# First projections of both mixers from rows not yet normalised, tokens' norm factors applied when the result is read out; the first layer's end in another order; one quarter of the output stored alone

## The chip, the core and the metric

The program runs on one core of one Trainium2 chip. Its time is the device time of one execution in microseconds (us). The kernel before takes 794.77 us, the median of three runs (793.01 to 795.64). All weights lie in HBM as fp32 and are read once: 240 MB in all.

## The reference

Two layers work on 272 tokens (16 learned meta tokens in front of 256 tokens of input) of width 1024. Each layer is a mixer and then a mixture of experts, both fed by an RMS norm and both added to the residual `h`:

```python
def rms_norm(x, gain):
    y = xf * lax.rsqrt(jnp.mean(xf * xf, axis=-1, keepdims=True) + NORM_EPS)
    return y * gain

# layer 0
p = rms_norm(h, e_norm) @ e_w_in                      # 1024 -> 2816
h = h + concat(rwkv7_mix(p[:, :1792]), rglru_mix(p[:, 1792:])) @ e_w_out
# layer 1
p = rms_norm(h, o_norm) @ o_w_in                      # 1024 -> 3088
h = h + gla_mix(p) @ o_w_out
# both layers
h = h + hier_moe(rms_norm(h, m_norm[layer]), ...)     # 32 experts of 256, 2 per token
# at the end
out = rms_norm(h, final_norm)[:, 16:]
```

The norm factor of a token is one number, and the gain is one number per channel of the model. A projection sums over channels, so the token's factor may be multiplied in before the projection or behind it, and the result is the same but for rounding. The gain has to be in before the sum. In `rwkv7_mix` each projected row is mixed with the row before it (`p + mu * (token_shift(p) - p)`); in `gla_mix` the first 512 columns of `p` are the queries, scaled by 1/sqrt(128).

## The kernel before, in words

Activations lie transposed: channels in the 128 partitions, tokens along the free dimension. A projection tile ("unit") is 128 output columns: 8 matmuls (k = 0 to 7, 128 channels each) that sum in one bank of PSUM (`ps`). Tokens are in three tiles: tile 0 and tile 1 are the 256 tokens of input, tile 2 the 16 meta tokens. The orders on all engines are written out by hand, each engine runs its own list in order, and semaphores tie the lists together (`s("xn")`, `s("acc")`, `s("vec_tr")` and so on).

**Entry of a mixer (`entry`, L1925 and L533).** TensorE transposes the rows of `H` into `ps`, bank k for channels of block k (`row_turn`, L1001). ScalarE squares and sums each row (in the second layer in two halves, `first_part` L520 and `second_part` L526), takes the root; VectorE inverts it and builds a diagonal matrix from it (`diag`, L1930). TensorE multiplies ones by that diagonal (`spread`, L1010), which puts each token's factor in all partitions, and ScalarE copies that to `rsB` (L547). Then VectorE makes the normalised, gained, transposed rows in eight instructions, `ps * gain * rsB` (L1937), and each frees one matmul of the first projection tile. The gains come as rows through a DMA (`gnr`), are transposed by TensorE (L1030) and copied to `gnT` by VectorE (L1934).

**First mixer.** `proj` (L1033) makes 22 tiles; ScalarE reads tile n out (`evac`, L551) as `raw` and as `mixed` (times 1 - mu), and VectorE adds the shifted part (`shift`, L1965). The mu and other small vectors (`pv`) come transposed behind tile 1 (L1066). VectorE clears several arrays between its L1937 and that copy (L1948 to L1954).

**Mixture of experts.** 8 turns of 4 experts; each turn's weights (gate, up, down: 4 MB each) come through four slots, so SyncE's queue of DMAs runs ahead as slots come free. The results are added to `H` through PSUM: TensorE's combines write a bank and VectorE adds it (`acc` counts these).

**The first layer's end (`experts(0)`, from L1631).** The last down weights come in pieces: columns 0 to 511 first, then the rest. TensorE makes the first half of y (`last_down(0, 512)`), combines it for tiles 2 and 0, makes the two quarters 512 to 767 and 768 to 1023, combines tile 1's first half, and then all second halves; VectorE adds, ScalarE squares. Behind that TensorE transposes all of `H`, and the entry of the second mixer follows. The second mixer's projection weights come in 13 groups (`O_GROUPS`) through five places of `wring`; its units are numbered 0 to 21 (units 0 and 1 are the first queries, unit 2 the gate's low-rank input).

**The end of the program.** Two halves of each row: the low half is scaled by GpSimd for tile 0 (L982) and by ScalarE for tile 1 (L913), the high half by VectorE (L2649). SyncE stores all of tile 0, ScalarE's queue all of tile 1.

## Time and profile before

| | before |
|---|---|
| median of three runs | 794.77 us (793.01 to 795.64) |
| the profiled execution, its own time | 795.4 us |
| its span on the profile's page | 792.7 us |
| TensorE matmuls, busy | 716.6 us (90%) |
| VectorE / ScalarE / GpSimd, busy | 319.1 / 205.6 / 30.8 us |
| read from HBM | 240.00 MB, 304 GB/s over the span |

The span is cut by what sets the pace. Mixer one ends at about 163 us, its experts at about 419, mixer two at about 534, its experts and the output take the rest. "Busy" of TensorE is high everywhere and doesn't tell a stage that waits for weights from one that doesn't; the share of the DMA engines and the first matmul of each stage do. All times below are us from the start of the span. An fp32 matmul has two records in the trace, a transpose has one.

### The profile page before, as it was taken

How to read it: one execution, taken by the hardware profiler on the slowest of the kernel's cores; microseconds unless marked ns; L12 is line 12 of the kernel's file. 1: busy time of each engine (PE TensorE's matmuls, PEld its weight loads, DVE VectorE, ACT ScalarE, POOL GpSimd, SP SyncE). 2: the span in 40 equal slices, each digit the busy share in tenths (PEclk: the TensorE clock that was granted, in tenths of full speed). 3: DMA queues.
4: the chain of work that ended last, by engine and by line, in shares of the span. 5: the costliest groups of instructions: out<-in, count | busy, mean ns of one | idle time of the engine just before them, and what ended most of it. 6: DMA issues, size and time to landing. Idle time of an engine off the chain costs nothing.

```text
span 792.7 us, 16704 instructions
## 1 busy us (share of the span) xinstructions
PE 716.6 (90%) x7436; PEld 456.6 (58%) x7436; DVE 319.1 (40%) x678; ACT 205.6 (26%) x414; POOL 30.8 (4%) x99
## 2 busy tenths in 40 slices
PE   8999999999989998999889999999998986877695
PEld 6778777658645564455537745884764543434342
DVE  6376876625353323333235054632445321221222
ACT  2574567215100000000032263540420000000003
POOL 7006000000000000000000000000000000000000
PEclk9999999999999998999999999999999998988998
DMA  8644113489999999999999613009999999999994
GB/s 261 197 104 141 55 55 110 166 342 378 396 421 420 421 420 421 420 420 421 411 330 370 225 62 102 1 8 408 421 386 422 420 421 420 421 420 421 421 403 159
DMA packets 69861, 242.14 MB, mean 305 GB/s; under 512 B 9814, under 2 KB 33484, under 8 KB 49052
## 3 DMA queue, kind: packets, MB, share of 16 engines
...
q10 hardware_dynamic: 208, 0.54, 0.2%
...
HBM read 240.00 MB, written 1.05 MB: 304 GB/s over the span
## 4 chain that ended last, share of the span: by engine, by line
PE 54%; DMA 17%; DVE 5%; issue 3%; SPq 1%; PEld 1%; ACT 0%; PEldq 0%; ACTq 0%
DMA M<-in_m_w_down_dram 12%; PE ps L1806 11%; PE ps L1499 10%; PE ps L1345 7%; PE ps L1446 6%; DMA M<-in_m_w_gate_dram 4%; PE ps L1461 4%; PE ps L1571 4%; DVE H L2403 1%; PE ps L1360 1%; PE ps L1639 1%; PE ps L996 1%; SPq L425 1%; PE ps L1380 1%; PE ps L1645 1%
## 5 line engine op out<-in xcount | busy, mean ns | idle before, releaser
L1499 PE MATMUL ps<-M 128*32 128x256 f32 x2016 | 127.3, 403 | 19.2 <-DMA M<-in_m_w_gate_dram 14.1
L1499 PEld LDWEIGHTS ps<-M 128*32 128x32 f32 x2016 | 67.3, 116 | 77.0 <-issue 19.4
L1806 PE MATMUL ps<-M 128*128 128x256 f32 (+2 forms) x320 | 87.0, 428 | 1.0 <-DVE M L1937 1.0
L1045 PE MATMUL ps<-M 128*128 128x272 f32 x352 | 85.0, 396 | 2.8 <-DVE M L2078 1.8
L1446 PEld LDWEIGHTS ps<-M 128*128 128x128 f32 x608 | 71.5, 192 | 12.4 <-issue 12.0
L1446 PE MATMUL ps<-M 128*128 128x128 f32 x608 | 76.9, 278 | 0.0
L1045 PEld LDWEIGHTS ps<-M 128*128 128x128 f32 x352 | 65.7, 190 | 18.3 <-issue 2.9
L1806 PEld LDWEIGHTS ps<-M 128*128 128x128 f32 x320 | 59.7, 190 | 24.5 <-issue 16.7
L1461 PE MATMUL ps<-M 128*128 128x512 f32 (+1 forms) x120 | 60.6, 626 | 7.4 <-DVE H L2403 5.3
L1571 PE MATMUL ps<-M 128*32 128x512 f32 x448 | 55.1, 636 | 13.0 <-DMA M<-in_m_w_down_dram 13.0
L2400 DVE TENSOR_TENSOR H<-H,ps 128x512 f32<-128x512 f32 x60 | 41.2, 687 | 61.2 <-PE ps L1461 60.9
L1345 PE MATMUL ps<-M 128*128 128x512 f32 (+1 forms) x160 | 57.5, 512 | 0.0
L2379 DVE TENSOR_TENSOR M<-ps,gm 128x512 f32<-128x512 f32 x28 | 19.4, 692 | 64.1 <-PE ps L1446 64.1
L1461 PEld LDWEIGHTS ps<-M 128*128 128x128 f32 (+1 forms) x120 | 19.0, 188 | 42.1 <-DVE H L2400 18.1
L797 ACT ACTIVATE M<-ps 128x272 f32<-128x272 f32 x16 | 6.4, 397 | 141.0 <-PE ps L1454 141.0
L1345 PEld LDWEIGHTS ps<-M 128*128 128x128 f32 x160 | 29.6, 190 | 23.0 <-issue 21.5
L795 ACT ACTIVATE M<-ps 128x256 f32<-128x256 f32 x16 | 6.1, 383 | 137.2 <-PE ps L1499 137.2
L1571 PEld LDWEIGHTS ps<-M 128*32 128x32 f32 x448 | 14.5, 116 | 42.7 <-issue 41.5
L2455 DVE COPY M<-ps 128x512 f32<-128x512 f32 x14 | 9.7, 692 | 58.2 <-PE ps L1571 58.2
L2403 DVE TENSOR_TENSOR H<-H,ps 16x256 f32<-16x256 f32 x32 | 13.2, 414 | 33.9 <-PE ps L1463 33.5
L803 ACT ACTIVATE M<-ps 128x512 f32<-128x512 f32 x16 | 9.6, 597 | 58.9 <-PE ps L1571 53.0
L982 POOL TENSOR_SCALAR M<-M,rs 128x512 f32<-128x512 f32 x1 | 1.6, 1567 | 555.0 <-DVE rs L1922 555.0
...
## 6 DMA issues: line engine op xcount, KB each, us to landing
...
M<-in_o_w_in_dram SPq DMA_DIRECT2D x12, 1024.0 KB, 8.9
M<-in_e_w_in_dram SPq DMA_DIRECT2D x11, 1024.0 KB, 6.0
M<-in_m_w_down_dram SPq DMA_DIRECT2D x9, 1024.0 KB, 18.4
M<-in_m_w_up_dram SPq DMA_DIRECT2D x8, 1024.0 KB, 18.6
M<-in_e_w_out_dram SPq DMA_DIRECT2D x4, 1024.0 KB, 5.3
```

Of the source, the lines that this page charges most:

```text
L803: nc.scalar.activation(yst[q % 2][:, 0:512], ps[:, 4, :], ACT.Copy).then_inc(s("ya"), 1)
L1045: ins = pe.matmul(ps[:, n % 4, 0:T], wringE[:, (n // 2) % 4, k, (n % 2) * P:(n % 2) * P + P], xnE[:, k], start=(k == 0), stop=(k == KD - 1))
L1345: ins = pe.matmul(ps[:, BANK[y][bank], 0:w], mixT[:, k, TOK[n]], w_out, start=(k == 0), stop=(k == 7))
L1446: ins = pe.matmul(ps[:, 1 + k // 4, (k % 4) * P:(k % 4) * P + P], xn[:, n, k, :], R[:, n, :], start=(n == 0), stop=(n == nt - 1))
L1461: return pe.matmul(ps[:, bank, :], rt_[:, TOK[n]], ys[:, 512 * hf:512 * hf + 512], start=True, stop=True)
L1499: ins = pe.matmul(ps[32 * e:32 * e + 32, 3 * x, 0:FF], xgT[q % 2][:, k, 32 * e:32 * e + 32], w, start=(k == 0), stop=(k == KD - 1))
L1571: ins = pe.matmul(ps[r, 4 + hf, :], hidT[:, k, r], dn_w[UNIT_SLOT[y][u]][:, e, k, 512 * hf:512 * hf + 512], start=(k == 0), stop=(k == 1))
L1806: ins = pe.matmul(ps[rows, unit % 4, 0:n], lhs(k), rhs(k), start=(k == 0), stop=(k == KD - 1))
L2379: return tt(xgT[q % 2][:, 4 * b:4 * b + 4], ps[:, 1 + b, :].rearrange("p (k t) -> p k t", k=4), gm[:, y, 4 * b:4 * b + 4].unsqueeze(2).to_ ...
L2400: return tt(H[:, n, c], H[:, n, c], ps[:, 6 + j % 2, :], ALU.add)
L2403: ins = tt(H[0:META, 2, c], H[0:META, 2, c], ps[32 * g:32 * g + META, 6 + j % 2, 0:256], ALU.add)
L2455: v.tensor_copy(yst[q % 2][:, 512:1024], ps[:, 5, :]).then_inc(s("yd"), 1)
```

## The change

1. **First mixer's entry.** The x rows of tile 0 are turned, then the gains, then tile 1 in two halves. VectorE makes `xuE = ps * gain` (no token factor) in two groups of four with the third inversion between them; projection tile 0 multiplies `xuE`, and `spread` stands in the middle of it. Behind it VectorE makes `xnE = xuE * rsB` in eight instructions, each of which frees one matmul of tile 1. The factor spread goes to banks 1 to 3 instead of 5 to 7. Tile 0 is read out by VectorE with `rsB` in it, into `raw` and `mixed`, and ScalarE starts with tile 1.
2. **First layer's end.** Tile 1's first half is combined at once, the first halves of tiles 2 and 0 are transposed before the two last quarters of y, tile 1's before the second halves are combined. ScalarE's copy of the last quarter stands behind all its three `first_part`.
3. **Second mixer's entry.** ScalarE makes k = 0 to 3 of `xuO = ps * gain`, VectorE k = 4 to 7. TensorE starts unit 0 with k = 0 and 1 before the other transposes, does k = 2 to 7 behind them, then `spread`, then unit 1 from `xuO` too. VectorE makes `xnO = xuO * rsB` in two instructions of 4x272 for the units from 2 on, and reads units 0 and 1 out with the factor in it (they were ScalarE's). VectorE's clearing of other arrays follows that.
4. **Output.** SyncE stores the high half of tile 0 when it is done and the low half when that is.

```diff
@@ -482,9 +485,10 @@
+            sp.dma_start(out[0, 0:P, 512:D], fin[:, 0, 512:D]).then_inc(s("st_out"), 16)
...
-            sp.dma_start(out[0, 0:P, :], fin[:, 0, :]).then_inc(s("st_out"), 16)
-            sp.wait_ge(s("st_out"), 32)
+            sp.dma_start(out[0, 0:P, 0:512], fin[:, 0, 0:512]).then_inc(s("st_out"), 16)
+            sp.wait_ge(s("st_out"), 48)
@@ -532,6 +536,10 @@
+                if y:
+                    act.wait_ge(s("vec_tr"), 5)
+                    for k in range(4):
+                        nc.scalar.activation(xuO[:, k], ps[:, k, 0:T], ACT.Copy, scale=gnT[:, 1, k:k + 1]).then_inc(s("xn"), 1)
@@ -544,7 +552,7 @@
-                    nc.scalar.activation(rsB[:, TOK[n]], ps[:, 5 + n, RBC[n]], ACT.Copy).then_inc(s("rb_set"), 1)
+                    nc.scalar.activation(rsB[:, TOK[n]], ps[:, ROOT_BANK[y] + n, RBC[n]], ACT.Copy).then_inc(s("rb_set"), 1)
@@ -553,7 +561,7 @@
-                    if n == 0:
+                    if n == 1:
@@ -578,7 +586,7 @@
-            evac(0)
+            act.wait_ge(s("proj_evac"), 1)
@@ -824,15 +832,18 @@
-                    if n == 1:
+                    if n == 1 and y == 1:
...
+                if y == 0:
+                    last_copy()
...
-            for n in range(22):
+            act.wait_ge(s("oproj_evac"), 2)
+            for n in range(2, 22):
@@ -1002,33 +1013,36 @@
-                        pe.transpose(ps[:, k, TOK[n]], H[:, n, k * P:(k + 1) * P], ident[:, :])
+                        ins = pe.transpose(ps[:, k, TOK[n]], H[:, n, k * P:(k + 1) * P], ident[:, :])
...
-                        pe.transpose(ps[:, k, TOK[n]], rows[:, k * P:(k + 1) * P], ident[0:META, 0:META])
+                        ins = pe.transpose(ps[:, k, TOK[n]], rows[:, k * P:(k + 1) * P], ident[0:META, 0:META])
+                return ins
...
-                    pe.matmul(ps[:, 5 + n, RBC[n]], ones[:, :], diag[:, P * n:P * n + cnt], start=True, stop=True) \
+                    pe.matmul(ps[:, ROOT_BANK[y] + n, RBC[n]], ones[:, :], diag[:, P * n:P * n + cnt], start=True, stop=True) \
...
-                pe.wait_ge(s("xn"), KD * y + k + 1)
+                pe.wait_ge(s("xn"), 2 * KD * y + k + 1)
...
-            for n in range(2):
-                pe.wait_ge(s(f"ld_x{n}"), 16)
-                row_turn(n, range(KD))
+            pe.wait_ge(s("ld_x0"), 16)
+            row_turn(0, range(KD))
...
-            spread(0, (0, 2, 1))
+            pe.wait_ge(s("ld_x1"), 16)
+            row_turn(1, range(4)).then_inc(s("vec_tr"), 1)
+            pe.wait_ge(s("dve_chain"), 3)
+            row_turn(1, range(4, KD)).then_inc(s("vec_tr"), 1)
@@ -1042,8 +1056,10 @@
+                    elif n == 1:
+                        pe.wait_ge(s("xn"), KD + k + 1)
...
-                                    xnE[:, k], start=(k == 0), stop=(k == KD - 1))
+                                    (xnE if n else xuE)[:, k], start=(k == 0), stop=(k == KD - 1))
@@ -1060,7 +1076,9 @@
-            proj(0)
+            proj(0, range(4))
+            spread(0, (0, 2, 1))
+            proj(0, range(4, KD))
@@ -1659,23 +1677,23 @@
+                    last_combine(1, 0, 7)
+                    pe.wait_ge(s("acc"), at0 + 1)
+                    row_turn(2, range(4))
+                    pe.wait_ge(s("acc"), at0 + 2)
+                    row_turn(0, range(4))
...
-                    pe.wait_ge(s("acc"), at0 + 1)
...
-                    pe.wait_ge(s("acc"), at0 + 2)
...
-                    last_combine(1, 0, 7)
+                    pe.wait_ge(s("acc"), at0 + 3)
+                    row_turn(1, range(4)).then_inc(s("vec_tr"), 1)
...
-                    row_turn(2, range(4))
-                    row_turn(0, range(4))
-                    pe.wait_ge(s("acc"), at0 + 3)
-                    row_turn(1, range(4))
@@ -1706,6 +1724,18 @@
+            def first_units(unit, ks):
...
+                for k in ks:
+                    if unit == 0:
+                        normed(1, k)
+                    ins = pe.matmul(ps[:, unit, 0:SEQ], wring[:, 0, k, unit * P:(unit + 1) * P], xuO[:, k, META:T],
+                                    start=(k == 0), stop=(k == KD - 1))
+                if ks[-1] == KD - 1:
+                    ins.then_inc(s("oproj"), 1)
...
+            pe.wait_ge(s("ld_w0"), 16 * (1 + 3))
+            first_units(0, (0, 1))
@@ -1715,9 +1745,11 @@
-            row_turn(1, range(4, KD))
+            row_turn(1, range(4, KD)).then_inc(s("vec_tr"), 1)
+            first_units(0, range(2, KD))
...
-            unit = 0
+            first_units(1, range(KD))
+            unit = 2
@@ -1768,7 +1800,7 @@
-            for g in range(len(O_GROUPS)):
+            for g in range(1, len(O_GROUPS)):
@@ -1790,8 +1822,8 @@
-                        if unit == 0:
-                            normed(1, k)
+                        if unit == 2 and k % 4 == 0:
+                            pe.wait_ge(s("xn"), 3 * KD + 1 + k // 4)
@@ -1922,20 +1954,23 @@
-            def entry(y, dst):
...
-                for n in (2, 0, 1) if y else (0, 2, 1):
-                    invert(2 * y, n)
-                    cnt = TILES[n][1]
-                    v.tensor_scalar(diag[:, 128 * n:128 * n + cnt], ident[:, 0:cnt], rs[:, 2 * y, n:n + 1], None, ALU.mult) \
-                        .then_inc(s("diag"), 1)
-                if y == 0:
-                    v.wait_ge(s("vec_tr"), 1)
-                    link(v.tensor_copy(gnT[:, :, :].rearrange("p n k -> p (n k)"), ps[:, 4, 288:320]))
-                v.wait_ge(s("rb_set"), 3 * y + 3)
-                for k in range(KD):
-                    stt(out=dst[:, k], in0=ps[:, k, 0:T], scalar=gnT[:, y, k:k + 1], in1=rsB, op0=ALU.mult, op1=ALU.mult) \
-                        .then_inc(s("xn"), 1)
+            def inverted(y, n):
...
+                invert(2 * y, n)
+                cnt = TILES[n][1]
+                v.tensor_scalar(diag[:, 128 * n:128 * n + cnt], ident[:, 0:cnt], rs[:, 2 * y, n:n + 1], None, ALU.mult) \
+                    .then_inc(s("diag"), 1)
...
+            def gained(y, dst, ks):
...
+                for k in ks:
+                    v.tensor_scalar(dst[:, k], ps[:, k, 0:T], gnT[:, y, k:k + 1], None, ALU.mult).then_inc(s("xn"), 1)
...
+            def over_tokens(*n):
+                b = rsB
+                for d in n:
+                    b = b.unsqueeze(1)
+                return b.to_broadcast([P, *n, T])
@@ -1943,7 +1978,19 @@
-            entry(0, xnE)
+            v.wait_ge(s("vec_tr"), 1)
+            link(v.tensor_copy(gnT[:, :, :].rearrange("p n k -> p (n k)"), ps[:, 4, 288:320]))
+            inverted(0, 0)
+            inverted(0, 2)
+            v.wait_ge(s("vec_tr"), 2)
+            gained(0, xuE, range(4))
+            inverted(0, 1)
+            v.wait_ge(s("vec_tr"), 3)
+            gained(0, xuE, range(4, KD))
+            v.wait_ge(s("xn"), KD)
+            v.wait_ge(s("rb_set"), 3)
+            for k in range(KD):
+                tt(xnE[:, k], xuE[:, k], rsB, ALU.mult).then_inc(s("xn"), 1)
@@ -1954,9 +2001,14 @@
-            v.wait_ge(s("vec_tr"), 2)
+            v.wait_ge(s("vec_tr"), 4)
...
+            v.wait_ge(s("pv_set"), 1)
+            v.wait_ge(s("proj_done"), 1)
+            tt(raw[:, 0, 1:T + 1], ps[:, 0, 0:T], rsB, ALU.mult)
+            stt(out=mixed(0), in0=ps[:, 0, 0:T], scalar=omm[:, E_TILES[0]:E_TILES[0] + 1], in1=rsB, op0=ALU.mult, op1=ALU.mult) \
+                .then_inc(s("proj_evac"), 1)
@@ -2515,8 +2567,7 @@
-                if y == 1:
-                    last_accumulate(1, 0, 7)
+                last_accumulate(1, 0, 7)
@@ -2525,19 +2576,31 @@
-                    last_accumulate(1, 0, 7)
...
-            entry(1, xnO[:, :, PAD:TP])
+            inverted(1, 2)
+            inverted(1, 0)
+            v.wait_ge(s("vec_tr"), 6)
+            v.wait_ge(s("xn"), 2 * KD + 4)
+            gained(1, xuO, range(4, KD))
+            inverted(1, 1)
+            v.wait_ge(s("xn"), 3 * KD)
+            v.wait_ge(s("rb_set"), 6)
+            for k in (0, 4):
+                tt(xnO[:, k:k + 4, PAD:TP], xuO[:, k:k + 4], over_tokens(4), ALU.mult).then_inc(s("xn"), 1)
+            for n in range(2):
+                v.wait_ge(s("oproj"), n + 1)
+                stt(out=qO[:, n, L:TP], in0=ps[:, n, 0:SEQ], scalar=float(P) ** -0.5, in1=rsB[:, META:T], op0=ALU.mult, op1=ALU.mult) \
+                    .then_inc(s("oproj_evac"), 1)
...
-            v.wait_ge(s("xn"), 2 * KD)
+            v.wait_ge(s("oproj_evac"), 2)
```

How the lists of instructions move, at the places that the prediction speaks of. First TensorE's list at the start of the program: transposes of `H` (of the 128 rows of x), the diagonals' spread (`ones`), and from L1045 the projection. Before:

```order
L1005 MATMUL ps<-ident,H 128x128 [waits ld_x0]
L1005 MATMUL ps<-ident,H 128x128 x7
L1005 MATMUL ps<-ident,H 128x128 [waits ld_x1]
L1005 MATMUL ps<-ident,H 128x128 x7
L1030 MATMUL ps<-ident,M 128x32 [waits ld_gn]
L1015 MATMUL ps<-M,ones 128x128 [waits diag]
L1015 MATMUL ps<-M,ones 128x16 [waits diag]
L1015 MATMUL ps<-M,ones 128x128 [waits diag]
L1045 MATMUL ps<-M 128x272 [waits xn,ld_w0]
L1045 MATMUL ps<-M 128x272 [waits xn] x7
L1045 MATMUL ps<-M 128x272 x8
```

After (L1061 is the projection):

```order
L1016 MATMUL ps<-ident,H 128x128 [waits ld_x0]
L1016 MATMUL ps<-ident,H 128x128 x7
L1041 MATMUL ps<-ident,M 128x32 [waits ld_gn]
L1016 MATMUL ps<-ident,H 128x128 [waits ld_x1]
L1016 MATMUL ps<-ident,H 128x128 x3
L1016 MATMUL ps<-ident,H 128x128 [waits dve_chain]
L1016 MATMUL ps<-ident,H 128x128 x3
L1061 MATMUL ps<-M 128x272 [waits xn,ld_w0]
L1061 MATMUL ps<-M 128x272 [waits xn] x3
L1027 MATMUL ps<-M,ones 128x128 [waits diag]
L1027 MATMUL ps<-M,ones 128x16 [waits diag]
L1027 MATMUL ps<-M,ones 128x128 [waits diag]
L1061 MATMUL ps<-M 128x272 [waits xn] x12
```

The gains' transpose now stands ahead of tile 1's, four matmuls of the projection stand ahead of the spread, and the wait for `xn` reaches over all 16. VectorE's list at the same place, where `M<-ps,gnT` are the gained rows. Before:

```order
L1922 RECIPROCAL rs<-rs 128x1 [waits sqr]
L1930 TENSOR_SCALAR M<-ident,rs 128x128 [waits rec]
L1934 COPY gnT<-ps 128x32 [waits vec_tr]
L1937 SCALAR_TENSOR_TENSOR M<-ps,gnT,M 128x272 [waits rb_set,dve_chain]
L1937 SCALAR_TENSOR_TENSOR M<-ps,gnT,M 128x272 x7
L1948 MEMSET M 128x4x3
L1949 MEMSET M 128x4
L1951 MEMSET M 128x4x48 x5
L1952 MEMSET K 128x1280
```

After:

```order
L1967 TENSOR_SCALAR M<-ps,gnT 128x272 [waits vec_tr]
L1967 TENSOR_SCALAR M<-ps,gnT 128x272 x3
L1954 RECIPROCAL rs<-rs 128x1 [waits sqr]
L1961 TENSOR_SCALAR M<-ident,rs 128x128 [waits rec]
L1967 TENSOR_SCALAR M<-ps,gnT 128x272 [waits vec_tr]
L1967 TENSOR_SCALAR M<-ps,gnT 128x272 x3
L1993 TENSOR_TENSOR M<-M 128x272 [waits rb_set,xn]
L1993 TENSOR_TENSOR M<-M 128x272 x7
L1995 MEMSET M 128x4x3
L1996 MEMSET M 128x4
L1998 MEMSET M 128x4x48 x5
```

Eight products with the factor (L1993) are added behind the eight with the gain. They stand ahead of the clears. Last, TensorE's list at the end of the first layer: `32x512` and `32x256` are the last down products, `16x256` and `128x512` the combines, `ident,H` the transposes and `M 128x256` the first units of the second mixer. Before:

```order
L1648 MATMUL ps<-M 16x256 [waits acc,ya,rt_set]
L1648 MATMUL ps<-M 16x256
L1645 MATMUL ps<-M 128x512
L1639 MATMUL ps<-M 32x256 [waits acc,ld_last1]
L1639 MATMUL ps<-M 32x256 x7
L1639 MATMUL ps<-M 32x256 [waits acc]
L1639 MATMUL ps<-M 32x256 x7
L1645 MATMUL ps<-M 128x512 [waits dn_last]
L1648 MATMUL ps<-M 16x256 [waits yl,yd]
L1648 MATMUL ps<-M 16x256
L1645 MATMUL ps<-M 128x512 x2
```

After:

```order
L1666 MATMUL ps<-M 16x256 [waits acc,ya,rt_set]
L1666 MATMUL ps<-M 16x256
L1663 MATMUL ps<-M 128x512 x2
L1019 MATMUL ps<-ident,H 128x16 [waits acc]
L1019 MATMUL ps<-ident,H 128x16 x3
L1016 MATMUL ps<-ident,H 128x128 [waits acc]
L1016 MATMUL ps<-ident,H 128x128 x3
L1657 MATMUL ps<-M 32x256 [waits ld_last1]
L1657 MATMUL ps<-M 32x256 x15
L1016 MATMUL ps<-ident,H 128x128 [waits dn_last,acc]
```

A combine and the first transposes now stand ahead of the last down products. Behind these rows the second halves' combines follow in both; before, the transposes, the spread and unit 0 come next, and after, as below:

```order
L1663 MATMUL ps<-M 128x512 x2
L1732 MATMUL ps<-M 128x256 [waits xn,ld_w0]
L1732 MATMUL ps<-M 128x256 [waits xn]
L1019 MATMUL ps<-ident,H 128x16 [waits acc,ld_lora]
L1019 MATMUL ps<-ident,H 128x16
L1019 MATMUL ps<-ident,H 128x16 [waits acc]
L1016 MATMUL ps<-ident,H 128x128 x3
L1019 MATMUL ps<-ident,H 128x16 [waits acc]
L1016 MATMUL ps<-ident,H 128x128 x5
L1732 MATMUL ps<-M 128x256 [waits xn] x6
L1027 MATMUL ps<-M,ones 128x16 [waits diag]
L1027 MATMUL ps<-M,ones 128x128 [waits diag] x2
L1732 MATMUL ps<-M 128x256 x8
```

Two matmuls of unit 0 went ahead of the later transposes, and six of unit 0 ahead of the spread.

## Rows read from the trace of the kernel before

**Rows 1.** Windows: busy us (x instructions) by engine, PEclk, DMA share, GB/s.

```profile
20.00:60.00 40.00, 39.91 (x187) 30.34 (x186) 22.56 (x49) 26.59 (x53) 1.39 (x10) 1.00 0.55 153
...
200.00:300.00 100.00, 92.35 (x950) 56.64 (x950) 37.63 (x86) 7.24 (x17) 0.53 (x1) 1.00 1.01 416
```

**Rows 2.** Timeline, TensorE, start of the program: start us, us, what.

```profile
5.81 3.54 PE L1005 MATMUL ps<-ident,H 128*128 128x128 f32 x16
...
9.46 0.94 PE L1015 MATMUL ps<-M,ones 128*128 128x128 f32 x6
11.46 7.57 PE L1045 MATMUL ps<-M 128*128 128x272 f32 x32 [1.06 <-DVE M L1937]
18.86 0.24 PE L1066 MATMUL ps<-ident,M 86*128 86x86 f32 x1
```

**Rows 3.** Timeline, VectorE and ScalarE, the same stretch.

```profile
10.81 3.36 DVE L1937 SCALAR_TENSOR_TENSOR M<-ps,gnT,M 128x272 f32<-128x272 f32 x8 [1.05 <-ACT M L547]
...
19.14 0.25 DVE L1958 COPY pv<-ps 128x86 f32<-128x86 f32 x1 [2.14 <-PE ps L1066]
...
30.18 0.40 ACT L561 ACTIVATE M<-ps 128x272 f32<-128x272 f32 x1 [2.89 <-PE ps L1045]
```

**Rows 4.** DMA queues in the window 0 to 7 us: packets, MB.

```profile
q10 hardware_dynamic: 64, 0.02, 1.7%
```

**Rows 5.** Groups by line and shape, VectorE: count, busy us, mean ns.

```profile
L2099 DVE TENSOR_TENSOR M<-M 128x272 f32<-128x272 f32 x4 | 1.8, 438 | 1.8 <-ACT M L572 1.8
...
L2147 DVE TENSOR_TENSOR M<-M 128x1088 f32<-128x1088 f32 x1 | 1.3, 1284 | 0.0
...
L2579 DVE TENSOR_SCALAR M<-ps,mq 128x256 f32<-128x256 f32 x1 | 0.5, 484 | 0.0
```

**Rows 6.** Timeline, GpSimd and VectorE, start of the program.

```profile
2.66 1.56 POOL L929 TENSOR_SCALAR_AFFINE_SELECT K<-ones 64x64 f32<-64x64 f32 x2
2.91 1.21 DVE L1942 TENSOR_TENSOR M<-M 16x1024 f32<-16x1024 f32 x1 [0.62 <-DMA M<-in_meta_dram]
...
4.50 0.24 POOL L929 TENSOR_SCALAR_AFFINE_SELECT id<-ones 64x64 f32<-64x64 f32 x1
```

**Rows 7.** Chain that ended last, first layer's end: start us, us, what.

```profile
409.60 0.61 PE ps L1648 x4
410.21 1.06 PE ps L1645 x2
411.27 1.93 PE ps L1639 x32
...
414.43 0.54 PE ps L1648 x4
...
416.88 0.35 PE ps L1008 x4
417.23 1.02 PE ps L1005 x8
...
419.87 0.46 PE ps L1015 x4
...
421.53 7.14 PE ps L1806 x32
428.68 1.04 PE ps L1797 x16
```

**Rows 8.** Timeline, ScalarE, first layer's end.

```profile
418.17 0.61 ACT L529 ACTIVATE M<-H 128x512 bf16<-128x512 f32 x1
```

**Rows 9.** DMA issues, 402.9 to 403.5 us: KB each, median us to landing.

```profile
M<-in_o_w_in_dram SPq DMA_DIRECT2D x1, 1024.0 KB, 11.3
```

**Rows 10.** Timeline, end of the program.

```profile
785.75 0.75 DVE L2649 SCALAR_TENSOR_TENSOR M<-ps,rs,H 128x512 f32<-128x512 f32 x1
...
787.45 0.36 SPq L486 DMA_DIRECT2D out_dram<-M  x1
```

**Rows 11.** DMA issues and bytes, 785 to 793 us.

```profile
GB/s 0 0 0 0 0 0 0 0 0 0 0 0 0 0 0 0 246 369 430 410 369 410 451 410 348 389 348 451 369 185 41 20 20 20 0 0 0 0 0 0
```

3 lines of the change are left out of this document (added).

## The prediction

> **What bounds the kernel now.** I read the windows by stage first. From 20 to 60 us TensorE is busy for 39.91 of 40 us and the DMA share is 0.55; in the experts (200 to 300 us) the share is 1.01 at 416 GB/s, and TensorE has gaps [rows 1]. So the mixers run at TensorE's pace and the experts at that of the weights. A stage of weights starts when the mixer ahead of it lets it, and the bytes are the same in both kernels. Hence a microsecond won at the entry of a mixer moves all behind it and is still there at the end, if nothing in between was late on its own. The question is how much earlier TensorE passes three places: the end of projection tile 1 at the start, the end of unit 2 in the second mixer, and the last store.
>
> At the start the timeline of TensorE shows transposes until about 9.4 us, the spread of the factors from 9.46, then a gap: the projection's first matmul is at 11.46, and 16 of them are through at 18.86, so one takes 0.46 us [rows 2]. The gap is the way diagonal, spread, ScalarE's copy, first product of VectorE. At the end of layer 0 the chain of waits is TensorE nearly alone: from 409.60 combines and last down products, second halves from 414.43 to 416.88, transposes behind them, and unit 0 at 421.53. Units 0 and 1 take 7.14 us (16 matmuls, 0.446 each), unit 2 1.04; it ends at 429.72 [rows 7].
>
> **The start.** Removed are the eight products with factor and gain (3.36 us of VectorE, 0.42 each [rows 3]); added are eight with the gain from PSUM, eight with the factor from SBUF, and two that read tile 0 out. The row for one source in PSUM is 0.484 for 256 columns alone, and 0.438 for two sources in SBUF of 272 [rows 5]; in a train the overlap takes some 0.07 off (3.36/8 against the 0.49 that one takes), so I count 0.42 for all.
> TensorE: transposes as before and one small one more in the middle, end 9.5. VectorE: tile 0 is turned at 5.81 + 8 x 0.22 = 7.6, the gains 0.2 later; copy 0.2, two inversions with their diagonals 0.8, so the gained rows start at 8.9 and the first is there at 9.3. The first matmul runs at 9.6 instead of 11.46. Four matmuls to 11.45; the third diagonal is ready at 8.9 + 4 x 0.42 + 0.5 = 11.1, so the spread needs no wait. It takes 0.94 alone [rows 2], less in a stream: 0.75. Twelve more matmuls, 5.55 us: tile 1 ends at 17.75, against 18.86. That is **1.1 us**, not the 1.9 of the first matmul, since the spread now stands in TensorE's way.
> Is VectorE in time? Gained rows to 12.8, the factors are there at about 12.7 (spread's end and 0.4), the eight products with the factor run 12.95 to 16.3, and TensorE wants the last at 17.3. Behind them the clears (about 3 us) and the copy of `pv`, which had 2.14 us of idle time ahead of it [rows 3]: it now comes at 19.2, as before. The read-out of tile 0 on VectorE then ends at 20.7, so ScalarE's tile 1 comes 0.3 later than before. That is covered: ScalarE waits 2.89 us for TensorE at the fifth tile (30.18 [rows 3]), and from there on it follows TensorE. Without that cover 0.3 would be lost. The gains must have landed by 7.6: all 64 packets of ScalarE's queue are done within the first 7 us [rows 4], so they have, by at least 0.6. Upper bound: the whole lead of 1.9. Lower bound 0, where tile 1 ends as before: VectorE's trains of 16 where there were 8 have room for 1.1 us.
>
> **The layer's end.** From 409.60, TensorE in its new order, each term from rows 7: meta combine 0.61, two combines 1.06 each, to 412.33; four meta transposes 0.35, four of tile 0 0.51, to 413.2; the two quarters 1.93 and their wait 0.14, to 415.26; four of tile 1 0.51, to 415.77; second halves 2.45, to 418.2 (before 416.88); two matmuls of unit 0 0.89, to 419.1; the other 12 transposes 1.6 (from 418.25 to the spread's last part at 419.87), to 420.7; six matmuls 2.68, to 423.4; the spread 0.6, to 424.0; unit 1 3.57, to 427.6; unit 2 1.04, to 428.6. Before: 429.72. So **1.1 us**: the gap from the spread to 421.53 is filled (1.2 with the spread's own drain), and 0.1 goes to the wait for the last quarter.
> What could be late instead? ScalarE's four copies go 415.8 to 417.1, before the second half of the meta rows has been added (about 417.2). VectorE's last half comes at 418.95. From the last square to the spread's end it was 2.2 us (418.17 [rows 8] to 420.33 [rows 7]), of which square and root are about 1.0, so the root is there at 420.0; VectorE makes k = 4 to 7 from 420.9 to 422.6 (TensorE wants k = 7 at 423.0) and the last diagonal at 423.1, 0.3 ahead of the spread. Queued behind that diagonal are only the two wide products: factors about 0.5 behind the spread, at 424.5, 1.28 each for 1088 columns [rows 5], so 425.8 and 427.1, and unit 2 asks at 427.6. The weights of unit 0 were issued at 402.95 and land 11.3 later, at 414.3 [rows 9], 3.9 before they are asked for. SyncE's wait for the last quarter, and behind it the issue of the output weights and of group 5, come about 2 us later; these are asked for behind unit 8 and at the end of the mixer, over 20 us on, and the same holds for the readers of what VectorE clears 4 us later. Bounds: 1.9 above (no spread in the way and no extra wait), -0.5 below (the roots 1.6 later than I have them; their slack is 0.3).
>
> **The output.** The high half of tile 0 is ready at 786.5, its store went at 787.45 with the low half [rows 10], and bytes flow from 788.2 to 791, about 1.05 MB at some 400 GB/s, with a few packets behind [rows 11]. Now 262 KB start 0.85 us earlier and are through when the rest starts; 786 KB stay, 0.65 us less. Packets of half the size may give some of it back: **0.5 us**, between 0 and 0.85.
>
> **Sum.** 1.1 + 1.1 + 0.5 = 2.7 us. Made against the profiled execution (span 792.7, 795.4 in all) it gives 792.7; that execution was 0.6 above the median of the runs, and against 794.8 it gives **792.1 us**.
>
> **Rivals.**
> *The early lead is lost in the first mixer* (1.6 us, 793.2). For it: behind 75 us TensorE, VectorE and ScalarE wait for each other in turn, and a chain of VectorE that did not start earlier would hold. Against: VectorE and ScalarE both idle before TensorE's tiles at 30 us [rows 3].
> *The late lead is lost* (1.6 us, 793.2): the third diagonal or the wide products come late. The margins are 0.3 and 0.5 us, a tenth of a train each; for it speaks that ScalarE now does the four copies ahead of its second squares.
> *Slower: VectorE and GpSimd get in each other's way at the start.* GpSimd builds masks until 20 us, and the added products with two sources in SBUF fall into that. The place: 12.95 us. The rows show that such a collision has a price: while VectorE multiplied two SBUF sources (2.91, 1.21 us), two of GpSimd's selects took 0.78 us each, against 0.24 at 4.50 [rows 6]. There GpSimd paid. If VectorE paid 0.78 for each of the eight, they would end at 12.95 + 8 x 1.2 = 22.55, tile 1 at 23.0 instead of 18.86: 4.1 lost, less the 1.6 of the two other places, 797.3. It decides from a product of 0.88 us on (12.95 + 8 x 0.88 + 0.46 = 20.45, which eats 1.6). Against: VectorE's 1.21 us for 1024 columns lies on the line through 0.438 for 272 and 1.284 for 1088 [rows 5], so it wasn't held; and GpSimd may be 3 us late, since the first wait for its masks (`pool_set` 2) stands behind the sixth tile, past 30 us. The Trainium skill, "GPSIMD Engine Reference", 1. Specifications, says that GpSimd's SBUF interfaces are shared with VectorE, with contention when VectorE's instruction has two SBUF inputs; it doesn't say who loses. By that rule alone the change would be charged for its eight products. By the rows the loser is GpSimd, and the charge is nothing. The trace agrees that there is contention.
>
> **How the numbers follow.** The forecast has 0.52 (own range 790.9 to 793.4), the early lead lost 0.15, the late one 0.15, slower 0.08, and 0.10 for what I haven't seen. A measurement of this kernel can tell 0.3%, 2.4 us, from no change; the forecast is 0.34%, just over it. So faster takes three quarters of the forecast, a fifth of the two half leads and some of the rest, about 0.50; within 0.38; slower 0.12. The range goes from both upper bounds nearly met (790.5) to 795.2, all gains lost; the slower case lies beyond it.
>
> **What would show it.** In the changed profile: the first projection matmul at about 9.6 us and the transpose of `pv` at about 17.8; a product of two SBUF sources at 0.44 us, GpSimd's masks done later than 20 us; tile 0 read out by 20.7; the same lead of 1.1 at the issue of the first expert weights. From the first combine of the layer's end to the end of unit 2 19.0 us instead of 20.1, no gap ahead of the spread. Last bytes 0.5 us sooner behind the last matmul. It is wrong if the lead at the first expert weights is 0, or if TensorE waits for VectorE in unit 0's six or in unit 2.

## The result

The changed kernel takes 788.6 us, the median of five runs (787.4 to 790.15), against 794.77 before. The ratio is 0.992 (95% interval 0.990 to 0.994): 6.2 us less, faster by more than the 0.3% that a measurement tells. Five single executions far off their fellows in the later comparisons (854.65 to 3999.31 us) are left out of all ratios. Forecast were 792.1 us, with a range from 790.5 to 795.2. The direction was right, the gain was more than twice what the sum gave, and the time lies outside the range.

| | before | after, profiled | after, run again, profiled |
|---|---|---|---|
| own time of the execution | 795.4 | 790.15 | 788.12 |
| span | 792.7 | 788.4 | 786.4 |
| projection tile 1 ends | 18.86 | 20.14 | 17.77 |
| first expert weights issued, layer 0 | 162.94 | 164.33 | 161.82 |
| first product of the last down weights, layer 0 | 405.41 | 404.98 | 403.23 |
| from there to the end of unit 2 | 24.24 | 21.43 | 21.43 |
| gate weights of layer 1 issued | 533.86 | 530.62 | 528.88 |
| last store issued | 787.45 | 784.66 | 782.62 |
| from there to the end of the span | 5.25 | 3.74 | 3.78 |

The last column is the experiment e5 below, the same kernel once more. From the end of unit 2 to the gate weights of layer 1 it is 104.21 us in before and after, 104.22 in e5, so nothing is lost or won in the second mixer. From the first expert weights to the first product of the last down weights of layer 0 it is 242.47, 240.65 and 241.41 us. This stretch is not alike in all profiles of this study: the seven kernels with the old order of the layer's end lie between 241.9 and 243.5 (mean 242.55), the eight with the new order between 240.4 and 242.3 (mean 241.28). The edits to the layer's end stand behind the stretch, and no run here shows why it should be 1.3 us shorter, so it is not counted as the change's below, and it stays open.

### The profile page after: what moved, and what is told of

Its sections match the earlier page's. It is cut to its first block, busy times and chain, and to the rows that moved or that the text cites. A ratio compares the mean times of both kernels' runs of the same rounds, so it can differ in the third digit from the quotient of the medians.

```text
span 788.4 us, 16720 instructions
## 1 busy us (share of the span) xinstructions
PE 716.0 (91%) x7436; PEld 457.0 (58%) x7436; DVE 324.4 (41%) x688; ACT 205.7 (26%) x414; POOL 31.4 (4%) x99
## 4 chain that ended last, share of the span: by engine, by line
PE 54%; DMA 17%; DVE 5%; issue 3%; SPq 2%; PEld 1%; ACT 0%; PEldq 0%; ACTq 0%
DMA M<-in_m_w_down_dram 13%; PE ps L1838 10%; PE ps L1517 10%; PE ps L1363 7%; PE ps L1464 6%; PE ps L1479 4%; DMA M<-in_m_w_gate_dram 4%; PE ps L1589 4%; DVE H L2455 1%; SPq L428 1%; PE ps L1378 1%; PE ps L1732 1%; PE ps L1007 1%; PE ps L1398 1%; PE ps L1657 1%
## 5 line engine op out<-in xcount | busy, mean ns | idle before, releaser
L1517 PE MATMUL ps<-M 128*32 128x256 f32 x2016 | 124.6, 396 | 20.1 <-DMA M<-in_m_w_gate_dram 11.6
L1061 PE MATMUL ps<-M 128*128 128x272 f32 x352 | 87.1, 403 | 1.9 <-DVE M L2130 1.8
L1838 PE MATMUL ps<-M 128*128 128x256 f32 (+2 forms) x288 | 79.9, 434 | 0.0
L1464 PEld LDWEIGHTS ps<-M 128*128 128x128 f32 x608 | 71.5, 192 | 12.5 <-issue 12.0
L1061 PEld LDWEIGHTS ps<-M 128*128 128x128 f32 x352 | 66.7, 193 | 18.0 <-DVE M L2130 1.9
L1589 PE MATMUL ps<-M 128*32 128x512 f32 x448 | 56.8, 653 | 12.7 <-DMA M<-in_m_w_down_dram 12.7
L1838 PEld LDWEIGHTS ps<-M 128*128 128x128 f32 x288 | 53.7, 190 | 22.6 <-issue 15.6
L1363 PEld LDWEIGHTS ps<-M 128*128 128x128 f32 x160 | 29.6, 190 | 23.0 <-issue 21.5
L2502 DVE TENSOR_TENSOR M<-M,ps 128x256 f32<-128x256 f32 x16 | 6.7, 420 | 43.6 <-PE ps L1517 43.6
## 6 DMA issues: line engine op xcount, KB each, us to landing
M<-in_m_w_gate_dram SPq DMA_DIRECT2D x32, 2048.0 KB, 17.8
```

The source lines that it names most:

```text
L1061: ins = pe.matmul(ps[:, n % 4, 0:T], wringE[:, (n // 2) % 4, k, (n % 2) * P:(n % 2) * P + P], (xnE if n else xuE)[:, k], start=(k == 0), s ...
L1363: ins = pe.matmul(ps[:, BANK[y][bank], 0:w], mixT[:, k, TOK[n]], w_out, start=(k == 0), stop=(k == 7))
L1464: ins = pe.matmul(ps[:, 1 + k // 4, (k % 4) * P:(k % 4) * P + P], xn[:, n, k, :], R[:, n, :], start=(n == 0), stop=(n == nt - 1))
L1517: ins = pe.matmul(ps[32 * e:32 * e + 32, 3 * x, 0:FF], xgT[q % 2][:, k, 32 * e:32 * e + 32], w, start=(k == 0), stop=(k == KD - 1))
L1589: ins = pe.matmul(ps[r, 4 + hf, :], hidT[:, k, r], dn_w[UNIT_SLOT[y][u]][:, e, k, 512 * hf:512 * hf + 512], start=(k == 0), stop=(k == 1))
L1838: ins = pe.matmul(ps[rows, unit % 4, 0:n], lhs(k), rhs(k), start=(k == 0), stop=(k == KD - 1))
```

## The profile after

**The start.** TensorE's timeline of after (start us, us, what). Its first matmul stands at 10.02, where [rows 2] had 11.46:

```profile
10.02 4.00 PE L1061 MATMUL ps<-M 128*128 128x272 f32 x8
13.81 0.99 PE L1027 MATMUL ps<-M,ones 128*128 128x128 f32 x6
14.64 5.67 PE L1061 MATMUL ps<-M 128*128 128x272 f32 x24
20.14 0.24 PE L1084 MATMUL ps<-ident,M 86*128 86x86 f32 x1
```

The first four matmuls (x8, two records each) take 4.00 us, 1.00 each, and the twelve behind the spread 0.47 each. The trace has no clock record ahead of 14.1 us in this execution; it begins there with the full 2.4 GHz (in before at 9.1). By their durations the four ran at half of that, at 1.2 GHz. The same rows of the same kernel in e5, where the record begins at 9.4 us:

```profile
9.70 2.07 PE L1061 MATMUL ps<-M 128*128 128x272 f32 x8
11.60 0.83 PE L1027 MATMUL ps<-M,ones 128*128 128x128 f32 x6
12.27 5.67 PE L1061 MATMUL ps<-M 128*128 128x272 f32 x24
17.77 0.24 PE L1084 MATMUL ps<-ident,M 86*128 86x86 f32 x1
```

So the four took 2.07 us and tile 1 ended at 17.77, 1.09 us before [rows 2]; in the first execution it ended 1.28 behind. A late rise isn't a matter of the new order. The kernel e6 below has the old start, its clock record begins at 17.8 us, and its tile 1 ended at 22.45:

```profile
12.33 10.28 PE L1045 MATMUL ps<-M 128*128 128x272 f32 x32 [1.06 <-DVE M L1936]
22.45 0.24 PE L1066 MATMUL ps<-ident,M 86*128 86x86 f32 x1
```

VectorE and GpSimd in e5, the rows that answer to [rows 3] and to the rival of [rows 6]:

```profile
12.85 3.00 DVE L1993 TENSOR_TENSOR M<-M 128x272 f32<-128x272 f32 x8
...
18.82 0.25 DVE L2005 COPY pv<-ps 128x86 f32<-128x86 f32 x1
...
19.31 0.44 DVE L2009 TENSOR_TENSOR M<-ps,M 128x272 f32<-128x272 f32 x1
19.67 0.49 DVE L2010 SCALAR_TENSOR_TENSOR M<-ps,omm,M 128x272 f32<-128x272 f32 x1
```
```profile
14.18 0.51 POOL L940 TENSOR_SCALAR_AFFINE_SELECT m_lev<-ones 64x32 f32<-64x32 f32 x1
14.76 0.64 POOL L940 TENSOR_SCALAR_AFFINE_SELECT m_lev<-m_lev 64x32 f32<-64x32 f32 x1
15.46 0.57 POOL L940 TENSOR_SCALAR_AFFINE_SELECT m_lev<-ones 64x32 f32<-64x32 f32 x1
16.11 0.30 POOL L940 TENSOR_SCALAR_AFFINE_SELECT m_lev<-m_lev 64x32 f32<-64x32 f32 x1
```

The eight products with two SBUF sources take 0.375 us each. GpSimd's selects have unlike durations in before too, so they must be held against the same ones in before. The second of these rows was there:

```profile
14.42 0.41 POOL L929 TENSOR_SCALAR_AFFINE_SELECT m_lev<-m_lev 64x32 f32<-64x32 f32 x1
```

It took 0.64 in e5 and 0.41 in before, its neighbours 0.51 and 0.57 instead of 0.42 and 0.33, and the one behind the products 0.30 in both. The charge falls on GpSimd.

**The layer's end.** TensorE's timeline of after. The bracket is the idle time ahead of the row and who ended it:

```profile
404.98 1.92 PE L1657 MATMUL ps<-M 128*32 128x512 f32 x16 [1.55 <-DMA M<-in_m_w_down_dram]
407.66 0.61 PE L1666 MATMUL ps<-M 128*16 128x256 f32 x4 [0.75 <-issue]
408.20 1.99 PE L1663 MATMUL ps<-M 128*128 128x512 f32 x4
410.11 0.42 PE L1019 MATMUL ps<-ident,H 16*128 16x16 f32 x4
410.46 0.66 PE L1016 MATMUL ps<-ident,H 128*128 128x128 f32 x4
411.05 1.93 PE L1657 MATMUL ps<-M 128*32 128x256 f32 x32
...
416.08 1.03 PE L1732 MATMUL ps<-M 128*128 128x256 f32 x4
...
421.15 0.83 PE L1027 MATMUL ps<-M,ones 128*128 128x16 f32 x6
421.82 3.62 PE L1732 MATMUL ps<-M 128*128 128x256 f32 x16
425.37 1.11 PE L1829 MATMUL ps<-M 128*16 128x272 f32 x16
```

No gap stands around the spread, where before had one up to 421.53 [rows 7]. From the first combine (407.66) to the end of unit 2 (426.41) it is 18.75 us; before it was 20.05. The last products now begin at once behind the transposes at 411.05, so their weights had landed. In before the same place reads (the row of L1639 at 411.23 is the last products):

```profile
405.41 3.43 PE L1639 MATMUL ps<-M 128*32 128x512 f32 x16 [1.90 <-DMA M<-in_m_w_down_dram]
409.60 0.61 PE L1648 MATMUL ps<-M 128*16 128x256 f32 x4 [0.76 <-issue]
410.14 1.13 PE L1645 MATMUL ps<-M 128*128 128x512 f32 x2
411.23 1.93 PE L1639 MATMUL ps<-M 128*32 128x256 f32 x32
```

Its first product took 3.43 us, not 1.92. The windows of before show why (TensorE busy, clock granted as a share of 2.4 GHz, DMA share, GB/s):

```profile
404.00:409.00 5.00, 3.43 (x16) 0.66 1.05 334
409.00:415.00 6.00, 5.23 (x45) 1.00 0.82 249
```

The granted clock was at 1.2 GHz for 3.4 us from 405.1, after TensorE had waited 1.90 us for these weights. In after it had waited 1.55, and the clock stayed up. How much of the slow product is on the path is told by the last piece of the weights, issued at 396.35 in before (KB, us from issue to landing):

```profile
M<-in_m_w_down_dram SPq DMA_DIRECT2D x1, 1024.0 KB, 14.6
```

It landed at 410.9, and the last products began at 411.23. With a faster first product they could have begun 0.3 us sooner and no more.

**The output.** DMA queues by packets, MB and share of 16 engines. First the two queues that after has in the window 783 to 789 us, then the one that only before has, in 785 to 793:

```profile
q1 hardware_dynamic: 288, 0.52, 23.2%
q10 hardware_dynamic: 144, 0.52, 22.2%
```
```profile
q14 instruction: 1, 0.01, 0.2%
```

Before has, beside the output's own packets, one of 8 KB that carries instructions, at 789.8 us. After has none there; its last packet of this queue starts at 745.5.

## The experiments

Each ran five rounds beside the kernel before. The stage tables below give us from the first product of the last down weights to the end of unit 2 ("layer's end") and from the last store's issue to the end of the span ("output").

**e1, the output quarter alone.**

```diff
+            sp.dma_start(out[0, 0:P, 512:D], fin[:, 0, 512:D]).then_inc(s("st_out"), 16)
-            sp.dma_start(out[0, 0:P, :], fin[:, 0, :]).then_inc(s("st_out"), 16)
+            sp.dma_start(out[0, 0:P, 0:512], fin[:, 0, 0:512]).then_inc(s("st_out"), 16)
```

> The kernel before with the output's part of the change alone: SyncE stores the high half of tile 0 as soon as it is done and the low half behind it. The prediction's theory: 0.5 us faster (ratio 0.9994). Rival, from the two profiles (last store's issue to the span's end 5.2 us before and 3.7 after, and 2.7 against 1.75 us outside the span): the output gives 1.5 to 2.5 us (0.997 to 0.998).

Ratio 1.0008 (0.9995 to 1.0021). Output 4.65 us instead of 5.25; the whole change has 3.74. So the quarter is worth 0.6 in the trace and isn't seen in the time, and 0.9 of the output's gain has another cause.

**e2, the start alone** (part 1 of the change; the rest as before).

> The first mixer's entry as changed, everything else as before. Prediction's theory: 1.1 us faster (0.9986), as long as the granted clock rises as early as in the profile before (9.1 us). Rival, from the profile of the changed kernel, where the clock was at 1.2 GHz until 14.1 us and tile 1 ended 1.3 us later than before: slower by up to 1.3 us (1.0016), if the new order itself makes the clock rise later. If the clock's rise moves by chance, the median stands near 0.9986 and the profile's clock and its tile 1 go together.

Ratio 0.998 (0.9969 to 0.9991), 1.6 us. First matmul 10.35 (it waited 0.75 us for the first projection weights; of the other runs only e7 waited there, 0.39 us), tile 1's end 18.45, layer's end 24.42, output 4.36. The output is 0.9 us shorter than in before though its part of the change is absent; e9 below shows why, and so the 1.6 us are not the start's alone.

**e3, the layer's end and the second entry** (parts 2 and 3).

> The first layer's end and the second mixer's entry as changed, start and output as before. Prediction's theory: 1.1 us faster (0.9986); 19.0 us from the first combine to the end of unit 2. Rival: the clock at the first down product (3.43 us at 1.2 GHz before, 1.92 at 2.4 after) belongs to the change, then 2.8 us (0.9965). If it is chance, this kernel's profile may show either.

Ratio 0.9974 (0.995 to 0.9998), 2.1 us, its times widely spread (788.8 to 797.9). Layer's end 22.66 with a first product of 2.99 us, partly at the low clock; output 4.44.

**e4, all but the output quarter.**

> The changed kernel with the output stored as before. If the parts add up to the changed kernel's 0.9922, this one is at 0.9922 plus the output's share: 0.9928 if the output gives 0.5 us, 0.9945 if it gives 1.8. The prediction's 2.2 us for start and layer's end would put it at 0.9972.

Ratio 0.9955 (0.9939 to 0.9971). Tile 1's end 18.15, layer's end 21.44, output 4.44.

**e5, the whole change again.**

> The changed kernel once more, beside the kernels of this group. If its first comparison (0.9922) was the change's own worth, it comes again. If the parts as measured so far are all there is (start 0.998, layer's end 0.9974, output about 1.000, and 0.9955 for start and layer's end together), it is at 0.995 to 0.9955. The prediction's 2.7 us would be 0.9966.

Ratio 0.9938 (0.9922 to 0.9955), 4.9 us. Against e4 the quarter is worth 0.66 us of output (4.44 to 3.78).

The next two ask whether the low clock at the last down weights is what before paid and after didn't.

**e6, before kept warm**: one matmul of 512 columns, used by nobody, ahead of the wait for the last down weights.

```diff
-                if y == 1:
-                    keep_busy(2, 4)
+                keep_busy(2 if y else 1, 4)
```

> The kernel before with one matmul of 512 columns on a free bank (1.1 us) in TensorE's wait for the last down weights of layer 0, which leaves out nothing and adds nothing to the result. Theory of the clock: in the profiles before and of three part kernels TensorE fell to 1.2 GHz for 3.4 us just as the weights landed (first down product 3.0 to 3.6 us), in two others it did not (1.92). If the fall comes from that wait, this kernel's product takes 1.92 us in the profile and the time falls by the 1.1 to 1.7 us in the executions that had the fall (ratio 0.998 to 0.999). Rival, the fall costs nothing that isn't hidden: ratio 1.0.

Ratio 1.0007 (0.9995 to 1.0018): nothing. TensorE's timeline of e6 says why:

```profile
408.59 1.92 PE L1639 MATMUL ps<-M 128*32 128x512 f32 x16
411.28 0.61 PE L1648 MATMUL ps<-M 128*16 128x256 f32 x4 [0.76 <-issue]
411.82 1.12 PE L1645 MATMUL ps<-M 128*128 128x512 f32 x2
413.98 1.93 PE L1639 MATMUL ps<-M 128*32 128x256 f32 x32 [1.03 <-DMA M<-in_m_w_down_dram]
```

The first product is 1.5 us shorter, and then TensorE waits 1.03 us for the two last quarters, which before had not waited for. The layer's end is 23.82 instead of 24.24. Even these 0.4 us are not the clock's. In e6 the weights of the first product, issued at 388.9, landed 19.2 us later, at 408.2, and the product began at 408.59 because the filler stood in its way. Counted from that landing the stage takes 24.3 us, and 24.4 in before (landing at 405.3).

**e7, after kept warm**, the same edit in the changed kernel.

> The changed kernel with the same filler matmul. If the change by itself keeps the clock up at the layer's end, the filler gives nothing (same ratio as the changed kernel beside it). If the two profiles without the fall were chance, it gives 0 to 1.5 us by the share of executions that fall, and its times scatter less.

Ratio 0.9931 (0.9914 to 0.9949), layer's end 21.44, output 3.77. The same as e5 within the measurement.

**e8, the order of the layer's end alone** (part 2, with the old entry).

> The kernel before with the layer's end in the new order alone (tile 1's combine and the first transposes ahead of the last down products), the second mixer's entry with normalised rows as before. By the prediction's way of counting the order alone moves 1.3 us of transposes from behind the second halves to ahead of them, where TensorE had only 0.1 us to spare, and gains nothing: the second halves come 1.3 us later, the last root too, ratio 1.001 (slower by about 0.5 to 1 us). Rival: the order is where the gain of the layer's end comes from, then 0.998.

Ratio 1.0012 (0.9995 to 1.0029), layer's end 25.06. The ratio is near the 1.001 expected, but not for the reason given, which was that the order gains nothing. A second effect takes the gain away. Its windows:

```profile
415.00:419.00 4.00, 2.82 (x18) 1.00 1.10 350
419.00:423.00 4.00, 4.00 (x12) 0.57 1.08 372
423.00:427.00 4.00, 4.00 (x20) 1.00 1.06 388
```

The clock was low for 3.4 us from 419.1, in units 0 and 1; TensorE had stood idle just before, 0.99 us for VectorE's first product. The two units took 8.83 us and not 7.14. The same 0.99 us stands ahead of unit 0 in before, e6, e9 and e12, where the clock stayed up there, so the wait alone doesn't explain the fall.

**e9, before with the code shifted.** Twelve one-column clears on VectorE in its idle time; they only make its code longer (the array `pad` is declared for them).

```diff
+            for i in range(12):
+                v.memset(pad[:, i:i + 1], 0.0)
             v.wait_ge(s("vec_tr"), 2)
```

> The kernel before with twelve more memsets of one column each on VectorE, put in its idle time at about 17 us, where nobody waits for them. They only lengthen VectorE's code. Theory of the output: an 8 KB packet of instructions that falls among the output's packets (it does in before, in the output quarter alone, and in two other runs, at 788 to 793 us) holds one DMA engine up by about 0.8 us; the added code moves it, so store issued to span's end is 4.4 us in place of 5.25, and the ratio is about 0.999. Rival: the 0.8 us has another cause, then it stays 5.2 to 5.3 us and the ratio is 1.000.

The packet of instructions left the output (it now starts at 776.7), and the output took 4.42 us instead of 5.25. (Its last store is issued at 787.68, its span ends at 792.1.) The ratio, 0.9995 (0.9978 to 1.0012), can't resolve 0.8 us of 794.

**e12, both**: e9 and the quarter alone.

> The same twelve memsets and the output's quarter stored alone, with nothing else of the change. Theory: store issued to span's end is 3.75 to 3.8 us as in the whole change (5.25 before), 1.5 us less in all, ratio about 0.998. Rival, that the output gains from the code or from the quarter but not both, or that the earlier stages of the change shortened it: 4.4 to 4.65 us as with the quarter alone, ratio 0.999 to 1.001.

Output 3.76 us, as in after; ratio 0.9991 (0.9976 to 1.0006), in which 1.5 us (0.9981) lies as well as nothing.

**e10, the second entry alone**, with the old order.

> The kernel before with only the second mixer's new entry (units 0 and 1 from rows not yet normalised); the order of the first layer's end is the old one. Before takes 24.2 us from the first product of the last down weights to the end of unit 2, order and entry together 21.4 (22.7 where the clock was low), order alone 25.1. Theory: the two only work together, since the old order leaves the first channel blocks' transposes to the very end of that stage, so the entry alone gives about 1 us or less: 23.2 to 24.2 us, ratio 0.999 to 1.0. Rival: the entry alone carries the gain, 21.4 to 22.2 us, ratio 0.997.

Ratio 0.9999 (0.9983 to 1.0014), layer's end 24.55. TensorE waited 1.53 us for the last quarters and 0.73 for ScalarE's copies ahead of unit 0, since the old order turns the rows only at the very end. The rival, that the entry alone carries the gain, is out.

**e11, the whole change started warmer**: three wide matmuls ahead of the first rows in place of one, the two narrow ones dropped. (The expectation below counts 13 in place of 6; the edit and the trace, with six records where after has two, show three and one.)

```diff
-            keep_busy(1, 7)
+            keep_busy(3, 7)
...
-            for _ in range(2):
-                pe.matmul(ps[:, 0, 384:512], ones[:, :], ones[:, :], start=True, stop=True)
```

> The whole change, with 13 wide matmuls that fill in front of the first rows in place of 6, and without the two narrow ones that followed the meta rows. Theory: in the profile of the changed kernel the clock was granted 2.4 GHz only at 14.1 us and the first four products took 4.0 us together, which cost 2.4 us against the execution in which it rose at 9.4; with TensorE busy longer and denser before its first transposes the rise comes at 9 us or sooner, projection tile 1 ends at 17.7 us or sooner, and the median is 0 to 1 us under that of the whole change, ratio about 0.992 to 0.994. Rival: the rise does not hang on what is done there, tile 1 ends between 17.8 and 20.1 us as before; or the added matmuls delay the first transposes, then tile 1 ends 0.5 to 1 us later and the ratio is 0.994 to 0.995.

Ratio 0.9953 (0.9935 to 0.997), no better. The clock's record begins at 5.2 us, but the first matmul then waits 0.75 us for VectorE, and tile 1 ends at 18.01, not before the 17.77 of e5: a rise earlier than e5's 9.4 won nothing. In this execution the changed kernel met the low clock at the layer's end instead, 6.8 us of it from 404.6, and lost all its gain of the layer's end (24.32 us). Its timeline and window (here with the clock as the share ahead of the last two numbers):

```profile
403.57 2.68 PE L1655 MATMUL ps<-M 128*32 128x512 f32 x16 [1.90 <-DMA M<-in_m_w_down_dram]
406.99 1.04 PE L1664 MATMUL ps<-M 128*16 128x256 f32 x4 [0.74 <-issue]
407.96 3.69 PE L1661 MATMUL ps<-M 128*128 128x512 f32 x4
...
412.52 1.93 PE L1655 MATMUL ps<-M 128*32 128x256 f32 x32
```
```profile
403.00:412.00 9.00, 7.68 (x29) 0.62 0.95 290
```

**e13, e8 kept warm**: one wide matmul as in e6, and three of 128 columns behind the spread, for which VectorE's fifth product of the entry waits.

```diff
+            for _ in range(3):
+                ins = pe.matmul(ps[:, 4, 384:512], ones[:, :], ones[:, :], start=True, stop=True)
+            ins.then_inc(s("rb_done"), 1)
             unit = 0
...
+                    if y == 1 and k == 4:
+                        v.wait_ge(s("rb_done"), 7)
```

> The order of the first layer's end alone, as before in that experiment, but with TensorE kept on matmuls whose result nobody uses: one wide one while it waits for the last down weights, three of 128 columns while it waits 0.99 us for VectorE ahead of the second mixer's unit 0. In the order alone the clock fell at 419.1 us, in unit 0, and units 0 and 1 took 8.83 us in place of 7.14. Theory: the order by itself is worth 1.1 us (from the first matmul of the two last quarters to unit 2's end 19.0 us, of which the clock took 1.7; before it is 18.4) and the fall of the clock takes it away again; kept on work, that stretch is 17.3 us, the stage from the first product of the last down weights 23.4, the ratio about 0.9985. Rival: the order is worth nothing by itself, then the stretch stays at 18.4 and the ratio at 1.000, whatever the clock does.

The layer's end took 23.39 us, the clock stayed up. TensorE's timeline of e13:

```profile
409.43 1.93 PE L1641 MATMUL ps<-M 128*32 128x256 f32 x32
...
417.48 0.83 PE L1722 MATMUL ps<-ones 128*128 128x128 f32 x6
418.63 7.14 PE L1810 MATMUL ps<-M 128*128 128x256 f32 x32 [0.33 <-DVE M L1943]
425.71 1.11 PE L1801 MATMUL ps<-M 128*16 128x272 f32 x16
```

From 409.43 to 426.75 it is 17.32 us, as expected, against 18.42 in before (411.23 to 429.65): the order by itself is worth 1.1. The same comes out of e8: 19.00 us from 409.60 to 428.60, less the 1.69 that the low clock took, are 17.31. The ratio, 0.9995 (0.9977 to 1.0013), doesn't confirm it and doesn't exclude it. A packet of instructions again fell into the output, which took 5.28 us.

## Why the prediction was off

**The start: mechanism right, the size at its upper end.** Predicted were the first matmul at 9.6 and tile 1's end at 17.75; e5 has 9.70 and 17.77. That is the best of the profiles with the new start: e11 has 18.01, e4 18.15, e7 18.20 and e2 18.45, on average 18.12 with e5, against 18.83 in the eight profiles with the old start and a clock record by 10.2. So the usual gain is 0.7 us, and the 1.1 of e5 is partly luck. The lead of 1.09 us is still 1.12 at the first expert weights. The masks ended later, at 21.2 instead of 20.4, and nobody waited. Tile 0 was read out by 20.2, half a us sooner than I had it. What I didn't count is that the place lies where the clock rises: 1.3 us lost in the profiled execution, 1.1 won in e5. The old start has the same risk, as e6 shows. That execution was the slowest of its five.

**The layer's end: mechanism right, the term mis-sized.** The step that failed is "From 409.60, TensorE in its new order, each term from rows 7" and with it "1.1 us". I took the first combine as the fixed point and priced each term behind it. By that measure the forecast holds: 19.0 against 20.1 predicted, 18.75 against 20.05 measured, so 1.3 of gain. But the fixed point lies elsewhere. The stage begins with the first product (24.24 to 21.43, 2.8 us), and the work moved ahead of the last quarters is free only where it stands in a wait. Split at the start of the last quarters:

| | first product | its start to the quarters | quarters to the end of unit 2 | sum |
|---|---|---|---|---|
| before, low clock | 3.43 | 5.82 | 18.42 | 24.24 |
| e12, old order, clock up | 1.92 | 6.21 (1.87 waiting) | 18.43 | 24.64 |
| e6, old order, kept warm | 1.92 | 5.39 (1.03 waiting) | 18.43 | 23.82 |
| after, e4, e5, e7 | 1.92 | 6.07 (none waiting) | 15.36 | 21.43 |
| e3, new order, low clock in part | 2.99 | 7.29 | 15.37 | 22.66 |
| e11, new order, low clock | 2.68 | 8.95 | 15.37 | 24.32 |

In the old order TensorE either ran the first product slowly or waited for the quarters: the two are the same 1 to 2 us, and taking one away uncovers the other (e6). The new order fills that wait with tile 1's combine and eight transposes. Behind it 3.06 us are gone in every run of the new order and entry together, of which e13 gives 1.1 to the order and leaves 2.0 to the unnormalised first units, and they need each other (e8, e10). The gain is 2.4 to 3.2 us where the clock stays up (2.7 at least where e6 is counted from the landing of its weights), 1.6 in e3 and nothing in e11, where it fell. The trace of before held both facts, the 3.43 us against 1.93 for as many columns, and the idle time ahead. I didn't look ahead of the first combine. What I had feared behind it came as counted: the third diagonal was ready 0.27 us ahead of the spread and the wide products 0.48 ahead of unit 2, where I had 0.3 and 0.5. So the rival of the lost late lead fell. ScalarE's last root of after, and then two rows of VectorE:

```profile
417.94 0.29 ACT L534 ACTIVATE rs<-ss 128x1 f32<-128x1 f32 x1
```
```profile
420.59 0.29 DVE L1961 TENSOR_SCALAR M<-ident,rs 128x128 f32<-128x128 f32 x1
422.40 2.49 DVE L2594 TENSOR_TENSOR M<-M 128x1088 f32<-128x1088 f32 x2 [1.52 <-ACT M L555]
```

The Trainium skill, "TensorE: Matmul & The Clock Gate", HAM oscillation, says that waiting for a DMA lets TensorE's clock fall, and charges the product run at the low clock with half its time. By it, an estimate, the slow product of before would cost 1.5 to 1.7 us. The trace agrees that the clock fell in a wait and that the product took 1.5 us longer. It doesn't agree that the time is lost: at most 0.3 us are on the path in before, where the last weights landed at 410.9, and e6 has a ratio of 1.0007.

**The output: the split right, a term missing.** The step that failed is "Packets of half the size may give some of it back" with the 0.5 us behind it, which had the stored bytes as the only term; the traces give 1.5. The quarter gives 0.6 to 0.66 us (5.25 to 4.65 in e1, 4.44 to 3.78 from e4 to e5), near the 0.65 counted ahead of the charge for small packets, which isn't there. The missing 0.8 us is the packet of instructions. Output took 5.23 to 5.31 us unsplit where it fell among the output's packets (before, e6, e8, e13) and 4.36 to 4.44 where it didn't (e2, e3, e4, e9, e10); split, 4.65 with it (e1) and 3.74 to 3.78 without. The packet goes with the length of VectorE's code: e9 lengthens nothing else and moves it out, e2, e3 and e10 lengthen that code too and have it ahead of their output, and e1, e6, e8 and e13 leave its length as it was but for one wait in e13, and keep it in. The change adds instructions to VectorE as well. How one packet holds the output up isn't shown. I had [rows 11] before me, in which bytes trickle for three slices behind the rest, and called them "a few packets behind".

**The sum.** 1.1 for the start as in e5, 2.8 for the layer's end and 1.5 for the output are 5.4 us, where I had 2.7; with the average start it is 5.0. The two comparisons give 6.2 (4.5 to 7.9) and, in e5, 4.9 (3.6 to 6.2), so either fits both. The 1.3 us by which the stretch ahead of the last down weights is shorter in kernels with the new order would lift the sum to the first comparison; whether they belong to the change isn't known. Measured one by one in time the parts give 1.6 (e2), 2.1 (e3) and 0.7 (e12), 4.4 together, uncertain by 0.9, 1.9 and 1.2. They can't be added up so: none of the three has the packet of instructions in its output, so its 0.8 us are in each of them, and with it counted once they leave 2.8, uncertain by about 2.4. What a single execution shows outside its span (2.7 us in before, 1.75 in after) is no part of it: nearly all profiles here have 1.7 to 2.0.

**The slower rival**, VectorE held up by GpSimd, is out by the rows above: 0.375 us per product. The Trainium skill, "GPSIMD Engine Reference", 1. Specifications, names the contention; the trace agrees, and shows who pays.

**What stays open.** How often the low clock meets each kernel isn't known, since only profiled executions show it. In the old order it did at the last down weights in before, e1, e2 and e9, and not in e10 and e12; in the new one in e3 and e11, and not in after, e4, e5 and e8. It went with TensorE's wait for these weights: the six profiles with the fall had waited 1.90 to 2.04 us, the six without it 0.76 to 1.77. What sets that wait in each execution isn't shown. In the old order the fall costs next to nothing and in the new one up to 2.9 us, so it may explain part of the spread of the times of e3 and e11; no run here separates it. No variant beat the changed kernel by what can be measured (e7 0.9931, e5 0.9938, the first comparison 0.9922).
